# A 31-tap convolution layer: from eight 256-channel chunks to sixteen 128-channel blocks on four PSUM banks

## What is computed

```python
h = rms_norm(x, norm_pre)
p = einsum('bsd,de->bse', h, w_pw1) + b_pw1          # 2048 -> 4096
g = p[..., :2048] * sigmoid(p[..., 2048:])
conv = causal depthwise conv of g, 31 taps, + b_dw    # per channel, over the 256 tokens
c = silu(layer_norm(conv, ln_g, ln_b))                # over the 2048 channels
y = einsum('bse,ed->bsd', c, w_pw2) + b_pw2
x = x + rms_norm(y, norm_post)
```

## Time and profile before

| | |
|---|---|
| median of 3 runs | 2074.62 us |
| profiled execution | 2073.36 us, span 2071.6 us, mean granted TensorE clock 0.994 |
| TensorE busy | 2033.2 us (98%) |
| VectorE busy | 1181.7 us (57%) |
| ScalarE busy | 987.6 us (48%) |
| GpSimd busy | 197.6 us (10%) |
| loads | 382.31 MB, mean 185 GB/s |

### The profile page before, as it was taken

How to read it: one execution, slowest core, us unless ns; L and a number is a source line. 1 busy time by engine, 2 the same in 40 slices (tenths; PEclk the granted TensorE clock), 3 DMA queues, 4 the chain that set the end, 5 groups by cost and what they waited for, 6 DMA issues and landing times.

```text
span 2071.6 us, 28886 instructions
## 1 busy us (share of the span) xinstructions
PE 2033.2 (98%) x10074; PEld 1724.3 (83%) x10074; DVE 1181.7 (57%) x1449; ACT 987.6 (48%) x1165; POOL 197.6 (10%) x118
## 2 busy tenths in 40 slices
PE   8999999999999999999999979999999999999998
PEld 6798888888888888888899968888888888888886
DVE  5745565555555544444599996565555555544444
ACT  5544464544455443433744475454444444443433
POOL 0000000000000000000688640000000000000000
PEclk9999999999999999999999989999999999999999
DMA  7735565555555555555355415565555555555554
GB/s 242 252 128 188 176 213 190 188 188 192 191 186 190 187 188 194 193 194 193 136 187 182 159 62 168 167 217 190 192 189 187 191 185 190 192 189 193 194 194 144
DMA packets 105128, 382.31 MB, mean 185 GB/s; under 512 B 11682, under 2 KB 12066, under 8 KB 104546
## 3 DMA queue, kind: packets, MB, share of 16 engines
q1 hardware_dynamic: 103968, 375.58, 54.3%
q0 software_dynamic: 944, 5.51, 0.8%
q10 hardware_dynamic: 148, 0.27, 0.1%
HBM read 379.21 MB, written 2.10 MB: 184 GB/s over the span
## 4 chain that ended last, share of the span: by engine, by line
PE 88%; DVE 8%; issue 3%; ACT 1%; DMA 1%; DVEq 0%; POOL 0%; SPq 0%; ACTq 0%
PE acc L1163 81%; DVE acc L1070 5%; PE acc L1174 1%; PE acc L1176 1%; PE acc L1175 1%; PE acc L1355 1%; DVE taps_now L1051 1%; PE acc L1213 0%; PE acc L1215 0%; DVE w_lo L785 0%; DMA vecs<-in_vecs 0%; DMA raw<-in_units 0%; ACT w_hi L463 0%; DVE conv L1072 0%; DVE acc L1065 0%
## 5 line engine op out<-in xcount | busy, mean ns | idle before, releaser
L785 DVE SCALAR_TENSOR_TENSOR w_lo<-raw,vecs,w_hi 128x1024 fp32r<-128x1024 f32 x400 | 512.7, 1284 | 474.7 <-ACT w_hi L463 472.7
L463 ACT ACTIVATE w_hi<-raw,vecs 128x1024 fp32r<-128x1024 f32 x400 | 459.9, 1153 | 525.1 <-PE acc L1163 491.4
L463 ACT ACTIVATE w_hi<-raw 128x1024 fp32r<-128x1024 f32 x304 | 322.7, 1064 | 460.5 <-PE acc L1163 358.5
L1163 PE MATMUL acc<-w_hi,xT_hi 128*128 128x512 f32 x1536 | 477.7, 392 | 5.3 <-DVE w_lo L785 4.7
L783 DVE TENSOR_TENSOR w_lo<-raw,w_hi 128x1024 fp32r<-128x1024 f32 x236 | 289.0, 1225 | 325.8 <-ACT w_hi L463 325.8
L1163 PE MATMUL acc<-w_lo,xT_hi 128*128 128x512 f32 x1536 | 473.8, 390 | 0.0
L1163 PE MATMUL acc<-w_hi,xT_lo 128*128 128x512 f32 x1536 | 473.3, 389 | 0.0
L1163 PEld LDWEIGHTS acc<-w_hi,xT_hi 128*128 128x128 f32 x1536 | 285.3, 188 | 66.9 <-issue 4.9
L1163 PEld LDWEIGHTS acc<-w_lo,xT_hi 128*128 128x128 f32 x1536 | 288.6, 188 | 60.5
L1163 PEld LDWEIGHTS acc<-w_hi,xT_lo 128*128 128x128 f32 x1536 | 288.6, 188 | 60.5
L1163 PE MATMUL acc<-w_hi,hT_hi 128*128 128x512 f32 x704 | 217.7, 389 | 0.0
(11 more groups left out here) (155 smaller groups left out, 1504.1 us busy)
## 6 DMA issues: line engine op xcount, KB each, us to landing
raw<-in_units SPq DMA_DIRECT2D x708, 512.0 KB, 3.3
gpost<-in_post POOLq DMA_DIRECT2D x4, 1024.0 KB, 6.1
x<-in_x SPq DMA_DIRECT2D x4, 512.0 KB, 8.0
out<-x SPq DMA_DIRECT2D x8, 256.0 KB, 2.8
tok<-in_lng POOLq DMA_DIRECT2D x1, 512.0 KB, 6.7
tok<-in_lnb POOLq DMA_DIRECT2D x1, 512.0 KB, 7.4
bs<-in_bs POOLq DMA_DIRECT2D x1, 256.0 KB, 7.9
taps<-in_taps ACTq DMA_DIRECT2D x1, 248.0 KB, 2.7
```

What stands on the lines that cost most here:

```text
L463: nc.scalar.activation(out, raw[:, s, :], ACT.Copy, scale=scale).then_inc(hi_ready, 1)
L785: ins = nc.vector.scalar_tensor_tensor(out[:, s, :], raw[:, s, :], vecs[:, gain:gain + 1], hi[:, s, :], ALU.mult, ALU.subtract)
L1163: last = mm(acc[:, 4 * par + 2 * t + h, :], xs, ws[:, s, h * BANK:(h + 1) * BANK], start=start and ws is w_hi and xs is xh, stop=stop and ...
```

## The change

The first product works in 16 chunks of one 128-channel block: 96 matmuls that fill one of four banks (`RING`), all written out without loops. The weights are reordered so that a unit holds four input blocks of one channel block.

- ScalarE makes only the sigmoid. VectorE gates in one instruction from the value half in PSUM (`ALU.add` of the bias, `ALU.mult` by the sigmoid), into a ring of four buffers. The copy of the value half, the copies of the taps and GpSimd's gates are gone.
- ScalarE begins the two chains of a block, taps 0 (with the bias) and 1, in the two halves of bank 4 or 5; VectorE runs taps 2 to 30, 29 instructions, even and odd taps in separate halves, and adds the two sums at the end of the block. The next block's gate is put behind tap 26 (tap 8 in the last block).
- VectorE convolves blocks 0 to 14, ScalarE and TensorE together block 15 only (31 products instead of 62).
- ScalarE's sequence per block: gate, split, begin taps (ahead of the next split in blocks 0 to 7, after it in 8 to 14), two splits. Squares and GpSimd's sums of channel pairs are interleaved with the first product.
- The opening: `spread_rs` moves to ScalarE, the transposed blocks are taken tile by tile in single blocks, the loads of taps and bias row go to SyncE's queue ahead of the layer's further weight loads, the sigmoid table is loaded early.
- TensorE sums the statistics behind the 31 products and runs 8 idle matmuls (`PE_WARM`) before and after the two spreads.

```diff
-            def gate(c, par):
-                split_quad(c * 2 + (Q_PW1 + 1))
...
-                    nc.scalar.activation(sig[:, par, n, :], acc[:, 4 * par + n, SEQ:2 * SEQ], ACT.Sigmoid,
...
-                    last = nc.scalar.activation(lin[:, par, n, :], acc[:, 4 * par + n, 0:SEQ], ACT.Identity,
...
+            def gate(n):
+                act.wait_ge(units_used, used_count(Q_PW1 + n, 3))
+                if n >= RING:
+                    act.wait_ge(glu_ready, n - RING + 1)
+                nc.scalar.activation(sig[:, n % RING, :], acc[:, n % RING, SEQ:2 * SEQ], ACT.Sigmoid,
+                                     bias=vecs[:, V_BG + n:V_BG + n + 1]).then_inc(sig_ready, 1)
+
+            def begin_taps(n):
+                act.wait_ge(glu_ready, n + 1)
+                act.wait_ge(taps_landed, 16)
+                if n >= 2:
+                    act.wait_ge(conv_ready, n - 1)
+                nc.scalar.activation(acc[:, 4 + n % 2, 0:SEQ], gated[:, n % RING, 0:SEQ], ACT.Identity, scale=taps[:, n, 0:1],
+                                     bias=vecs[:, V_BDW + n:V_BDW + n + 1]).then_inc(taps_begun, 1)
+                nc.scalar.activation(acc[:, 4 + n % 2, SEQ:2 * SEQ], gated[:, n % RING, 1:1 + SEQ], ACT.Copy,
+                                     scale=taps[:, n, 1:2]).then_inc(taps_begun, 1)
...
+            for n in range(LAST):
+                gate(n)
+                split(Q_PW1 + n + 1, 3)
+                if n < INIT_LATE:
+                    begin_taps(n)
+                split(Q_PW1 + n + 2, 0)
+                if n >= INIT_LATE:
+                    begin_taps(n)
+                split(Q_PW1 + n + 2, 1)
+                if n >= 3 and n % 2:
+                    square_pair((n - 3) // 2)
+                split(Q_PW1 + n + 2, 2)
+            gate(LAST)
+            split(Q_PW2, 3)
+            square_pair(PAIRS - 1)
...
+            def glu(n):
+                dve.wait_ge(sig_ready, n + 1)
+                if n >= RING:
+                    dve.wait_ge(conv_ready, n - RING + 1)
+                nc.vector.scalar_tensor_tensor(gated[:, n % RING, PAD:], acc[:, n % RING, 0:SEQ], vecs[:, V_BA + n:V_BA + n + 1],
+                                               sig[:, n % RING, :], ALU.add, ALU.mult).then_inc(glu_ready, 1)
+
+            def convolve(n, next_at):
+
+                for j in range(2, TAPS):
+                    i = j - 2
+                    m = acc[:, 4 + n % 2, (j % 2) * SEQ:(j % 2 + 1) * SEQ]
+                    if i == 0:
+                        dve.wait_ge(taps_begun, 2 * n + 2)
+                    elif i > 1:
+                        dve.wait_ge(tap_done, n * (TAPS - 2) + i - 1)
+                    out = conv[:, n, :] if j == TAPS - 2 else m
+                    nc.vector.scalar_tensor_tensor(out, gated[:, n % RING, j:j + SEQ], taps[:, n, j:j + 1], m,
+                                                   ALU.mult, ALU.add).then_inc(tap_done, 1)
+                    if j == next_at:
+                        glu(n + 1)
+                dve.wait_ge(tap_done, (n + 1) * (TAPS - 2))
+                nc.vector.tensor_tensor(conv[:, n, :], conv[:, n, :], acc[:, 4 + n % 2, 0:SEQ], ALU.add).then_inc(conv_ready, 1)
+
+            glu(0)
+            for n in range(LAST):
+                convolve(n, 8 if n == LAST - 1 else 26)
```

More of the change, by code:

```diff
@@ L46 @@
 FFC = DFF // BANK
-CC = 256
-CCH = D // CC
+CCH = D // P
+RING = 4
+LAST = CCH - 1
+PE_WARM = 8
 Q_V = 0
@@ L1408, in _ @@
-            conv_in(0, 0, False)
-            conv_in(1, 1, False)
-            with pe.Fori(1, CCH // 2) as i:
-                pe.wait_ge(gate_ready, i * 2 - 1)
-                conv_in(i * 2, 0)
-                pe.wait_ge(gate_ready, i * 2)
-                conv_in(i * 2 + 1, 1)
+            for c in range(CCH):
+                if c >= RING:
+                    pe.wait_ge(glu_ready, c - RING + 1)
+                for s in range(4):
+                    pe.wait_ge(lo_ready_pool, lo_pool_count(Q_PW1 + c, s))
+                    for kk in range(4):
+                        k = 4 * s + kk
+                        if c == 0:
+                            pe.wait_ge(xc_lo_ready, conv_parted(1, k))
+                        for half in range(2):
+                            last = block_by_channel(s, (2 * kk + half) * P, k, c % RING, half, k == 0, k == KT - 1)
+                    last.then_inc(units_used, 1)
@@ L1427, in sum_channels @@
-            def sum_channels(n, values, squares, ready, squares_ready):
-                for square in range(2):
-                    pe.wait_ge(*(squares_ready if square else ready))
-                    for b in range(2):
-                        src = squares[:, b, :] if square else values[:, b, :]
-                        for t in range(T):
-                            last = mm(acc[:, 6, 2 * t + square:2 * t + square + 1], src[:, t * P:(t + 1) * P], one_mean[:],
-                                      start=n + square + b + t == 0, stop=n == 2 and b == 1, skip_group_check=True)
-                last.then_inc(sq_summed, 1)
@@ L1439, in _, with sum_channels @@
-            pe.wait_ge(consts_set, 5)
-            by_pool = (sq_added, 2 * (SQ_POOL - 1))
-            sum_channels(0, conv_sum, sq_sum, by_pool, by_pool)
-            for n in (1, 2):
-                place = SQ_POOL - 1 + n
-                c = SQ_ORDER[place]
-                sum_channels(n, conv[:, 2 * c:2 * c + 2, :], sq[:, place % 2],
-                             (conv_last_ready, 2) if c == CCH - 1 else (conv_ready, 2 * (c + 1)), (sq_ready, place + 1))
+            def sum_channels(values, squares, first, stop):
+                for square, src in enumerate((values, squares)):
+                    for t in range(T):
+                        last = mm(acc[:, 7, 2 * t + square:2 * t + square + 1], src[:, t * P:(t + 1) * P], one_mean[:],
+                                  start=first and square + t == 0, stop=stop, skip_group_check=True)
+                return last
@@ new lines, in _ @@
+            pe.wait_ge(consts_set, 4)
+            pe.wait_ge(sq_added, 2 * (PAIRS - 1))
+            for b in range(2):
+                last = sum_channels(conv_sum[:, b, :], sq_sum[:, b, :], b == 0, False)
+            last.then_inc(sq_summed, 1)
+            pe.wait_ge(conv_ready, LAST)
+            pe.wait_ge(sq_last_ready, 1)
+            sum_channels(conv[:, LAST - 1, :], sq_last[:, 0, :], False, False).then_inc(sq_summed, 1)
+            pe.wait_ge(conv_last_ready, 1)
+            pe.wait_ge(sq_last_ready, 2)
@@ L1451, in _ @@
+            for n in range(PE_WARM):
+                mm(acc[:, 5, 0:P], ones[:], ones[:], start=True, stop=True)
             for j in range(2):
```

275 lines of the change are left out of this document (105 added, 170 removed).

## The result

| | before | after |
|---|---|---|
| median (4 runs each, same chip) | 2074.94 us (2074.54 to 2075.31) | 2055.89 us (2054.81 to 2057.50) |
| ratio | | 0.9907, 95% interval 0.9892 to 0.9923 |
| profiled execution | 2073.36 us, span 2071.6 | 2054.9 us, span 2053.2 |
| TensorE busy | 2033.2 us (98%) | 2017.8 us (98%) |
| VectorE busy | 1181.7 us (57%) | 1165.6 us (57%) |

The kernel is 19 us faster (0.9%); the forecast, 2053.8, was 2 us too low. Nearly all of the gain is in the one stage. The stage begins 1.4 us later in the profile of after; in the profiles of all thirteen kernels tried here, whose code up to there is nearly the same, that point lies between 990.8 and 993.0 (990.81 and 992.45 in two whose code there is that of before).

What follows compares the result with a forecast made beforehand. VectorE's taps and tap copies were taken to bound the convolution stage. The second product 20.2 us earlier plus 0.6 made 20.8, so 2052.6 us profiled, 1.26 below the median forecast of 2053.8; range 2046.5 to 2063.

Steps and rivals of the forecast that it cites:

- VectorE's blocks: Convolution layer: 29 taps at 0.392 us, a gate of 0.39 and an add, 12.25 us per block, bounds 12.1 and 13.2.
- Rival 1: GpSimd holds VectorE's new gate and add as it held the old gate: 13 us more, 2067 us; chance 0.06.
- Rival 3: Even and odd tap chains in one bank run one after another, pitch at least 0.54: +64 us, 2118; chance 0.03.
- The opening: Start of the convolution layer: first product at 1004.3 us (bounds 1003.3 and 1006), VectorE's first tap at 1018.5.
- the cover: Opening: next weight unit lands at 1008.8 us, ScalarE wants it at 1008.9; no margin, up to 1 us lost.
- 4 x 0.45: Opening: sigmoid, gate and two beginnings of about 0.45 us each, from the first sigmoid at 1016.1 to VectorE's first tap.
- TensorE's loss at block 15: End of the first product: TensorE loses about 0.5 us to late weight splits, so that product ends at 1189.1.
- the slack 5.6 - 0.73n: Spare us for weight splits behind ScalarE's waits at block n: 0.5 at n = 7, -0.5 to -1 at n = 13.
- rival 2: Weights come late, TensorE stalls, block 15's gate holds the last chain: 4 to 9 us, 8 likely, 2062; chance 0.12.
- The end of the stage: After block 14 starts (1190.0): products from 1193.9 to 1209.1, sums to 1213.9, then 5.7 us to the second product at 1219.6.
- The second product: Before, half clock lost 2.5 us at its start; now the same or a 1.5 us wait; 1.9 taken, gain 0.6.
- The sum: Whole kernel: 20.8 us gained, 2052.6 us for a profiled execution, 1.26 below the median.

## Why the prediction was right, and where it was off

Step by step, in us from the last matmul ahead of the layer (the prediction counted from 990.81):

| step | predicted | measured |
|---|---|---|
| first matmul of the layer | 13.5 | 12.5 |
| VectorE's first tap | 27.7 | 27.7 |
| period of a block | 12.25 | 12.23 |
| block 14 starts | 199.2 | 198.9 |
| gate 15 done | 202.5 | 202.1 |
| products begin | 203.1 | 202.7 |
| products end | 218.3 | 217.8 |
| last sum ends | 223.1 | 222.6 |
| second product | 228.8 | 229.8 |
| rest, against before | -0.6 | -0.6 |

- **VectorE's blocks** were right in every term, to 0.1 us: taps at 0.392 to 0.395, gate and add as if GpSimd did nothing. Rival 1 was wrong; the two-SBUF gate shows that its mechanism is real for the other form. Rival 3 was wrong, and the taps in series show what it would have cost (an extra 0.13 us for each tap).
- **The opening** had errors that cancel, so the hit at 27.7 is in part luck. The first matmul was 1 us earlier: 0.3 from the second diagonal, the rest as the clock was up for the second tile. ScalarE lost 0.72 us to a late load (at 1010.68), where I had put the cover at nothing and up to 1 us lost. The terms from the sigmoid to the first tap, 4 x 0.45, give 1017.9 and not the 1018.5 written; 2.29 us were measured, as a split stands between sigmoid and beginnings. TensorE's 1.08 us at 1020.43, which VectorE did not feel, have a second cause that the prediction lacks: VectorE's subtraction of the bias row, 2.28 us with two SBUF sources, held GpSimd's split, 3.54 us instead of 2.40.
- **TensorE's loss at block 15** didn't come; the only wait of the first product was that 1.08 at 1020.43. The step that failed is the slack 5.6 - 0.73n, which has too little at its start: the beginning stands late from block 8 on, and there was no wait for a low part from then on. With all beginnings early the losses came two blocks later than the formula has them, about 0.7 a block in four blocks, and cost 0.7 to 1.0 us of the stage at most, as VectorE's blocks come last. For that reason rival 2 (TensorE stalls, block 15 late) also had less in it than the 0.12 that I gave it.
- **The end of the stage**: 5.7 us from the last sum to the second product were 7.2. This is the term of the sum that was mis-sized, within its bounds of 5.3 to 8. I stayed near full clock for it (5.3), with the idle matmuls at 1.6 us, and had 3.2 for half clock: the clock fell behind the sums and they took 3.52. Without them the stretch was 5.98. Why the clock falls in the sums isn't shown: in after it was 1.00 up to 1214 and 0.73 in 1214 to 1216, in the kernel with the bias behind the sums, which has no idle matmuls there, 0.62 already in 1212 to 1214, and with the filler ahead of the products 0.89 in 1212 to 1214.
- **The second product** had full clock and the new wait, 1.12 us where I had 1.5, and the rest came out 0.6 shorter, as I took it.
- **The sum**: stage 1.0 late (1.5 from this term, -0.5 from the ones before), start of the stage 1.4 late, which is no effect of the change; 2052.6 + 2.4 = 2055.0, where the profiled execution had 2054.9. The median is 1.0 above that; I had 1.26.

Where the 19.2 us of the stage came from, by the runs: taking the beginnings off VectorE gives 12.7, the gate's form 5.1. The copies, removed alone, brought VectorE's end 12.5 us forward and the time only 6.0, because TensorE's two last blocks were next. These are prices in different kernels and do not add up to 19. What the smaller chunk gives by itself, one block at each end instead of two, wasn't tried and stays open. The opening's diagonals have no share that the runs could see.

## What to carry to other kernels

When an engine's relief is to be priced, work out which chain is second latest where they meet: here 12.5 us less on VectorE were worth 6 as long as two blocks were left to TensorE, and what came through whole were the terms on VectorE once one block was left. A filler that keeps the clock pays only where what follows can use the time: alone it gave nothing, and with the last block shared it gave about 2 us (2.6 by the medians, 1.9 of the stage). Idle matmuls in the queue ahead of one that others wait for are a cost at the clock that they run at, so put real work there (the bias rows) and keep the count small.

## What the runs showed of the hardware

- The hold between GpSimd and a VectorE instruction with two SBUF sources goes either way: the same 128x256 gate took 0.41 to 0.42 us free and 1.01 to 2.09 held, and a GpSimd split took 2.74 us beside a gate and 3.54 beside a bias subtraction, instead of 2.40. A diagonal that started 0.07 us ahead of a GpSimd split had its full speed (0.28); one that started 0.49 behind it took 1.94.
- A VectorE tap that waits for its direct predecessor has a pitch of 0.525 us, one that waits for the tap before that one 0.392; two alternating halves of one PSUM bank are enough for that.
- The granted clock fell to 0.50 during or right behind 32 records of one-column matmuls. In after TensorE had worked without a pause for 20 us by then, and the next 16 records of 128 columns took 3.52 us, where I had taken 1.6 at full clock.
